# A quarter of the tokens taken out of the dense expert sweep and gathered row by row

## What is computed

```python
idx = e1 * PEER_KEYS + e2                      # 128 tokens x 8 heads x 16
gate = jax.nn.softmax(sc, axis=-1).astype(hb.dtype)
u_sel = u_tab[idx]
v_sel = v_tab[idx]
act = jax.nn.gelu(jnp.einsum('td,thkd->thk', hb, u_sel), approximate=False) * gate
return jnp.einsum('thk,thkd->td', act, v_sel)
```

## Time and profile before

| what | value |
| --- | --- |
| median of 3 runs | 4597.31 us (4595.19 to 4605.93) |
| span of the profiled execution | 4622.7 us, its own time; 0.55% above the median |
| TensorE busy | 94% of the span |
| VectorE, ScalarE, GpSimd busy | 56%, 32%, 42% of the span |
| first to last way-down matmul | 1366.5 to 2707 us of the span |

### The profile page before, as it was taken

The page is one execution under the profiler, slowest core; times in us unless marked ns, Lnnn a source line. Parts: engine busy times, 40 slices in busy tenths (PEclk is TensorE's granted clock), DMA queues, the critical chain, the costliest instruction groups (busy, mean ns, idle before and its releaser), DMA issues.

```text
span 4622.7 us, 51856 instructions
## 1 busy us (share of the span) xinstructions
PE 4338.2 (94%) x20942; PEld 3385.7 (73%) x20942; DVE 2596.0 (56%) x4411; ACT 1498.9 (32%) x2478; POOL 1942.0 (42%) x1058
## 2 busy tenths in 40 slices
PE   7989999998799999999999989988999989989998
PEld 4767755477678888888888866676888867656886
DVE  4785744369857888878544352644434350365334
ACT  4212211035853222222222233553222231353222
POOL 3155332047964555555444433003223226434443
PEclk9989999998899999999999999998999999999999
DMA  7100300332354444444554320001222212102331
GB/s 266 44 23 20 118 30 28 136 112 99 142 205 152 164 167 164 160 164 157 178 166 156 119 69 19 16 15 51 64 64 63 64 34 64 42 1 78 96 93 53
DMA packets 171050, 445.52 MB, mean 96 GB/s; under 512 B 12251, under 2 KB 79003, under 8 KB 167612
## 3 DMA queue, kind: packets, MB, share of 16 engines
q1 hardware_dynamic: 168060, 422.61, 27.3%
q0 software_dynamic: 2752, 19.60, 1.1%
HBM read 404.41 MB, written 37.75 MB: 96 GB/s over the span
## 4 chain that ended last, share of the span: by engine, by line
PE 72%; DVE 3%; POOL 3%; ACT 3%; issue 2%; DMA 0%; POOLq 0%; ACTq 0%; DVEq 0%
PE psum L254 20%; PE psum L256 20%; PE psum L255 20%; PE psum L260 11%; POOL o L1813 1%; PE psum L355 1%; POOL Pe L2685 1%; POOL Pd L2687 1%; DVE o L1696 0%; DVE X L2076 0%; POOL pair L244 0%; ACT o L1765 0%; ACT stage L1771 0%; ACT o L1762 0%; ACT P L2468 0%
## 5 line engine op out<-in xcount | busy, mean ns | idle before, releaser
L244 POOL TENSOR_TENSOR pair<-raw_ring,pair 128x1024 fp32r<-128x1024 f32 x502 | 1306.2, 2611 | 1949.9 <-ACT pair L236 1897.4
L236 ACT CAST pair<-raw_ring 128x1024 fp32r<-128x1024 f32 x502 | 516.1, 1046 | 742.2 <-PE psum L256 708.2
L254 PE MATMUL psum<-pfh,pair 128*128 128x512 f32 x1152 | 459.1, 399 | 4.5 <-DVE pfl L1589 3.5
L255 PE MATMUL psum<-pfl,pair 128*128 128x512 f32 x1152 | 458.0, 398 | 0.0
L256 PE MATMUL psum<-pfh,pair 128*128 128x512 f32 x1152 | 457.9, 397 | 0.0
L1881 DVE SCALAR_TENSOR_TENSOR hlate<-psum,mods,hlate 128x512 f32<-128x512 f32 x512 | 367.8, 748 | 154.2 <-PE psum L256 154.1
L254 PE MATMUL psum<-Ah,pair 128*128 128x512 f32 x1024 | 408.1, 398 | 4.0 <-DVE Al L1875 4.0
L255 PE MATMUL psum<-Al,pair 128*128 128x512 f32 x1024 | 407.8, 398 | 0.0
L256 PE MATMUL psum<-Ah,pair 128*128 128x512 f32 x1024 | 407.8, 398 | 0.0
L254 PE MATMUL psum<-ffh,pair 128*128 128x512 f32 (+1 forms) x1056 | 379.5, 359 | 25.9 <-DVE ffl L2047 15.7
L255 PE MATMUL psum<-ffl,pair 128*128 128x512 f32 (+1 forms) x1056 | 378.5, 358 | 0.0
(11 more groups left out here) (620 smaller groups left out, 8826.7 us busy)
## 6 DMA issues: line engine op xcount, KB each, us to landing
raw_ring<-wmod SPq DMA_DIRECT2D x144, 512.0 KB, 5.5
raw_ring<-peeru SPq DMA_DIRECT2D x128, 512.0 KB, 3.5
raw_ring<-peerv SPq DMA_DIRECT2D x128, 512.0 KB, 3.8
gates<-stage SPq DMA_DIRECT2D x16, 2048.0 KB, 6.6
Gb<-gates SPq DMA_DIRECT2D x32, 1024.0 KB, 9.4
raw_ring<-win SPq DMA_DIRECT2D x48, 512.0 KB, 4.4
raw_ring<-wgate SPq DMA_DIRECT2D x44, 512.0 KB, 3.5
raw_ring<-wup SPq DMA_DIRECT2D x44, 512.0 KB, 3.6
```

The lines of the kernel that those rows point to most:

```text
L236: ac.e.copy(self.pair(t)[0], k.R.of(t)).then_inc(*k.A.up("hi", t))
L244: po.e.tensor_tensor(lo, k.R.of(t), hi.bitcast(F), ALU.subtract).then_inc(*k.G.up("lo", t))
L254: e.matmul(out, w[0], x[0], start=first, stop=False, skip_group_check=True)
L255: e.matmul(out, w[0], x[1], start=False, stop=False, skip_group_check=True)
```

## The change

The last 128 of the 512 tokens leave the dense sweep. `DENSE` is 384.

1. Route: only 96 spreads (three blocks of tokens) instead of 128. For block 3 the expert numbers are written as integers to `row16`, one column for each of its 128 choices, and the block's normalised tokens are turned to rows in `htok` (16 matmuls, two copies).
2. Way up: 8 trios of 384 columns. Its bank is one of two (6 and 7); from tile 17 on the gelu is written back into the bank, and so is the product with the gates (`gelus`, `products`). The gate chunks are 384 wide too.
3. Way down: the roles are turned. 128 tokens of `Ah`/`Al` are the weights, 512 columns of V are streamed; three token blocks by two halves, 18 matmuls of 512 columns a tile, summed over all 128 tiles in six banks. The 512 additions into `hlate` are gone.
4. Rows: for the last 128 tokens, partition = token. GpSimd issues an indirect DMA for each of the 128 choices from the U table and, later, each of the 128 from the V table: 128 rows of 4 KB, 512 KB each, into one of four buffers. VectorE reduces a U row against `htok` (one number per token, first half, groups 0 to 30), and accumulates a V row times its number in `acc` (groups 32 to 62). They are four, at times five a group (128 over 31 groups). GpSimd issues the rows of group `gi+1` in its group `gi`, each after VectorE is done with the row four before it.
5. End: six banks are copied out, 32 transposes bring the tokens back to columns, eight additions into the residual, which is now loaded into `X` once tile 127 is through the way up.

```diff
+DENSE, CHUNKS, SPREADS = 384, 12, 96
...
-    for u in range(128):
+    for u in range(SPREADS):
...
+    def down(n):
+        hi, lo = W.pair(("V", n))
+        pe.wait_ge(W.split(("V", n)), V.at("A", n))
+        for tt, hf in SIDES:
+            ts, hs = slice(128 * tt, 128 * tt + 128), slice(512 * hf, 512 * hf + 512)
+            i = trio(e, B.of(("dense", tt, hf)), (k.Ah[n % 4][:, ts], k.Al[n % 4][:, ts]), (hi[:, hs], lo[:, hs]), n == 0, n == 127)
...
-            project(k, pe, ("U", n), k.px, SEG1)
-        down(gi)
+            project_in(k, pe, ("U", n), k.ux, SEGU, None, (6, 7))
+        down(2 * gi)
+        down(2 * gi + 1)
...
+    def row(s):
+        x = k.sel_rows[s % 4]
+        dv.wait_ge(k.rowl[s % 4].at(s // 4 + 1))
+        if s < 128:
+            dv.wait_ge(A.at("htok", 1))
+            e.tensor_tensor_reduce(x, x, k.htok, 1.0, 0.0, ALU.mult, ALU.add, k.act1[:, s:s + 1]).then_inc(*V.up("row", s))
+            return
...
+        e.scalar_tensor_tensor(out=k.acc, in0=x, scalar=a, in1=k.acc, op0=ALU.mult, op1=ALU.add).then_inc(*V.up("row", s))
...
-        if gi == 63:
-            vector_affine_scale(k, dv, "ev", k.mods2[0], 0, SEG2, P.at("used", ("U", 127)))
-        down(gi)
+            for s in rows[2 * i:2 * i + 2] if i == 0 else rows[2:]:
+                row(s)
...
+    def row(s):
+        po.wait_ge(V.at("row", s - 4) if s > 3 else V.at("rows"))
+        table = k.d["peerrow"] if s < 128 else k.d["peerv"].rearrange("a b c -> (a b) c")
+        at = bass.IndirectOffsetOnAxis(ap=k.row16[:, s % 128:s % 128 + 1], axis=0)
+        e.indirect_dma_start(out=k.sel_rows[s % 4], out_offset=None, in_=table, in_offset=at).then_inc(*k.rowl[s % 4].up())
+
+    for s in chosen_rows(0)[0:4]:
+        row(s)
```

More of the change, by code:

```diff
@@ L1430 @@
 NO, FIRST, EARLY, AHEAD = 4, 8, 14, 17
+DENSE, CHUNKS, SPREADS = 384, 12, 96
+SEGU = [(0, DENSE)]
+SIDES = tuple((tt, hf) for hf in range(2) for tt in range(3))
+GROUPS = 31
 BESIDE = {2: 8, 34: 9, 66: 10}
@@ L1532, in deal @@
     cost, load, out = {"pool": 0.84, "scalar": 0.87, "vector": 0.29}, {"pool": 0.0, "scalar": 0.0, "vector": 0.0}, []
-    for u in range(128):
-        load["vector"] += CHOICE if u < 96 else 0.68
+    for u in range(SPREADS):
+        load["vector"] += CHOICE
         load["scalar"] += 0.58
@@ L1670, in choose @@
         V.name("esel", tt)
+        if tt == 3:
+            dv.wait_ge(V.now())
+            e.scalar_tensor_tensor(out=place, in0=k.esel[:, 0:128], scalar=128.0, in1=k.esel[:, 128:256], op0=ALU.mult, op1=ALU.add).then_inc(*V.up())
+            dv.wait_ge(V.now())
+            e.tensor_copy(k.row16, place).then_inc(*V.up("rows"))
         dv.wait_ge(A.at("gexp", tt))
@@ L1689, in vector_route @@
     dv.wait_ge(V.now())
-    for u in range(128):
+    for u in range(SPREADS):
         tt, n = u // 32, u % NO
         if u % 32 == 0:
-            nxt = choose(tt + 1) if tt < 3 else iter(())
+            nxt = choose(tt + 1)
             dv.wait_ge(V.at("EG", tt))
@@ L1704, in vector_route @@
         next(nxt, None)
-        if u % 32 == 28 and tt < 3:
+        if u % 32 == 28 and tt < 2:
             chosen(tt + 1)
+    for _ in nxt:
+        pass
     V.name("end", "route")
@@ L1772, in spread @@
         B.over(("sp", u), A.now())
+    ac.wait_ge(k.hkeep.at())
+    for hf in range(2):
+        ac.wait_ge(P.at("ht", hf))
+        e.copy(k.htok[:, 512 * hf:512 * hf + 512], B.of(("ht", hf))).then_inc(*A.up("htok", hf))
+        B.over(("ht", hf), A.now())
     choose(0)
-    for u in range(128):
+    for u in range(SPREADS):
         if u in BESIDE:
@@ L1875, in up @@
         e.tensor_tensor(k.Al[n % 4], y, k.Ah[n % 4].bitcast(F), ALU.subtract).then_inc(*V.up("A", n))
[L1877 to L1883, removed]
+        if n >= AHEAD:
+            B.over((("U", n), 0), V.now())
+    def row(s):
[5 more added lines that the diff above has]
+            return
+        a = k.act2[:, s - 128:s - 127]
+        if s == 128:
+            dv.wait_ge(A.at("gelu", "rows"))
+            e.tensor_tensor(k.act2, k.act2, k.gate, ALU.mult).then_inc(*V.up())
+            dv.wait_ge(V.now())
+            e.tensor_scalar(k.acc, x, a, None, ALU.mult).then_inc(*V.up("row", s))
+            return
+        dv.wait_ge(V.at("row", s - 1))
+        e.scalar_tensor_tensor(out=k.acc, in0=x, scalar=a, in1=k.acc, op0=ALU.mult, op1=ALU.add).then_inc(*V.up("row", s))
     def mods(t):
@@ L1971, in pool_experts @@
     for gi in range(NG):
+        rows = [s for s in chosen_rows(gi + 1) + (chosen_rows(gi + 2) if gi + 1 == GROUPS else [])] if gi != GROUPS else []
+        rows = iter(rows)
         for n in ups(gi):
             W.lo(po, ("U", n))
+        for s in rows if gi < 8 else ():
+            row(s)
         for n in (2 * gi, 2 * gi + 1):
+            for s in range(2):
+                nxt = next(rows, None)
+                if nxt is not None:
+                    row(nxt)
             W.lo(po, ("V", n))
+        for s in rows:
+            row(s)
     G.name("end", "experts")
     po.wait_ge(k.V.at("A", 127), k.P.at(("U", 127), 0))
+    e.dma_start(k.X[:, :, 0:512], k.d["hkeep"]).then_inc(*k.hkeep.up())
     e.dma_start(k.X[:, :, 512:768], k.d["ctxT2"]).then_inc(*k.ctxl.up())
@@ L3547, in sync_program @@
     R.load(sp, ("U", FIRST + 7))
-    for ch in range(16):
+    for ch in range(CHUNKS):
         sp.wait_ge(A.at("sp", 8 * ch + 7))
```

150 lines of the change are left out of this document (98 added, 52 removed).

## The result

The changed kernel takes 4432.92 us (median of 4, 4423.59 to 4440.32) against 4598.14 us for the kernel before on the same chip (median of 4). The ratio is 0.963 (95% interval 0.961 to 0.966): 165 us less. Forecast were 4414 us and a ratio of 0.960; the range was 4290 to 4585. In the two profiled executions the spans differ by 191 us (4622.7 and 4431.5). Up to the first scaling of the next block (L2889, now L2992) it is 178 (it starts at 2713.53 and 2535.76); the other 13 lie in later stages with the same instructions in both. That they are the change's is not shown: from that instruction to the end the trace of before takes 1909 us, those of the changed kernel and its eight variants 1889 to 1902. One wait of TensorE of 9.2 us, near 3215, stands in the trace of before and not in that of after; why is open.

The account below looks back on a forecast made before the run. The prediction took TensorE to bound the expert sweep, but not the route, before the change. Sweep -138, route and start -54 and end +9 gave -183 us, from a median of 4597 to 4414 us; range 4290 to 4585.

Parts of the forecast that it names:

- TensorE's price: Expert sweep: matmul time is proportional to columns, 0.176 us for 384; a group of two tiles takes 16.85 us.
- VectorE and the port, groups 8 to 40: Sweep: VectorE's 14.4 us of work plus 6.8 of waits for GpSimd give 21.0 us a group, bounds 19.2 and 23.8.
- Groups 41 to 61: Later sweep: 18.5 us a group with single modulation sums (41 to 56), TensorE's 16.85 with none (from 57).
- Groups 0 to 7: Start of the sweep: VectorE's work and the turning row buffers give 12.2 us a group, 98 us, bounds 80 and 115.
- Group 31 and the rest: Group 31, without rows, takes TensorE's 16.85 us; the whole sweep sums to 1200 us, 138 less.
- fifth rows: Sweep, 8 groups with a fifth row: GpSimd waits into VectorE's next group, 1 us lost each, 8 us.
- Route and start: Before the sweep: 47.3 us of spreads go, 2.41 of wait and 8.2 of ways up saved, issues cost 3.5; together -54.
- End: After the last way down: bank copies, transposes, additions and GpSimd's squares cost +9 us; residual's load has 12 us of cover.
- Rival 1: Sweep: VectorE and GpSimd take turns at the port without cost, TensorE stays the bound; 4221 us, chance 0.10.
- Rival 2: Sweep: an issue and a port operation exclude each other, about 3.5 us a group more on VectorE; 4582 us, chance 0.18.
- Rival 3: Sweep: indirect issues are long, GpSimd becomes the bound; break-even at 2.4 us an issue, 4704 us at 3; chance 0.12.
- Rival 4: Sweep: idling TensorE gets a clock of 0.80, costing up to 3 us in 22 groups, 66; no chance of its own.

Follow-up runs that it names:

- experiment 2: The changed kernel without any gathering of rows and without the rows' arithmetic (256 one-column operations in its place): 4227.61 us, ratio 0.918.
- experiment 1: The changed kernel with the arithmetic of the gathered rows cut to 128 of 1024 columns, every gather and wait kept: 4302.72 us, ratio 0.933.
- experiment 3: The changed kernel with each indirect DMA replaced by a plain GpSimd DMA of 128 neighbouring rows, same bytes and waits: 4392.43 us, ratio 0.954.
- experiment 4: The changed kernel with GpSimd's subtraction cut to 512 of 1024 columns for expert tiles above 40: 4313.44 us, ratio 0.937.
- experiment 5: The changed kernel with GpSimd's list reordered from group 8 on, each subtraction followed by one row issue: 4421.50 us, ratio 0.961.
- experiment 6: The changed kernel with two GpSimd subtractions put before the four first issues and the residual's load issued by ScalarE: 4420.84 us, ratio 0.960.

## Why the prediction was right

The forecast was right in sign, in the mechanism of groups 8 to 40 and nearly in size: 4414 against 4433. Part of the closeness is luck, as terms that were off by 5 to 20 us stand against each other. Point by point:

**TensorE's price.** The way-up matmuls of 384 columns start 0.174 us apart (0.176 taken from half and full width). With nothing beside them a group takes 16.7 us (16.85), experiment 2.

```profile
1603.46 0.34 PE L254 MATMUL psum<-pfh,pair 128*128 128x384 f32 x1
1603.64 0.34 PE L255 MATMUL psum<-pfl,pair 128*128 128x384 f32 x1
1603.81 0.34 PE L256 MATMUL psum<-pfh,pair 128*128 128x384 f32 x1
```

**VectorE and the port, groups 8 to 40.** Forecast: 14.4 us of own work (1.4 of it for ScalarE's rounding) and 6.8 of waits inside instructions, rounded down from 21.2 to 21.0. Measured in groups 8 to 30: instructions of 20.0 us a group, of which 7.3 are above the least length of their kind (5.3 in row sums, 1.9 in modulation sums), so 12.7 of work, and 1.1 of waiting for ScalarE's rounding between; the overlap of ends and starts takes some of it back, and the period is 20.3. A tile's two operations take 0.56 us each; 0.62 was taken. The waits came out at 1.8 a subtraction (1.7 forecast), though in another pattern. The prediction expected row sums at 1.22 or 3.3 us, few between; of the 128 row sums 58 took under 1.35 us, 22 about 1.85 (they met the end of a subtraction), 42 about 3.4, and 6 from 5 to 10, through several subtractions. Experiments 1, 3 and 4 together show that VectorE's work and its waits for the subtractions set the pace, experiment 2 what is left without them.

The Trainium skill ("SBUF — State Buffer", "SBUF: two separate sides") says that whichever starts first keeps the pair for the whole instruction. The trace agrees for a single one. That a waiting VectorE operation was let in only after three of GpSimd's subtractions (1600.38 to 1607.46) goes beyond what that sentence says.

**Groups 41 to 61** were forecast at 18.5 and 16.85 and took 19.2 and 17.8: +16 us together. What was mis-sized is GpSimd's list. The forecast had 1.1 us an indirect issue and its own waits at the port only in subtractions. Measured are 1.37 in the mean (0.93 least; the rest is mostly the wait for VectorE's port operation) and 0.3 us of gap before the next issue. Per group of 41 to 56, 4 x 2.60 + 4.1 x 1.40 + 4.1 x 0.3 = 17.4 us. That is above TensorE's 16.7, but 2.9 of it are waits for VectorE inside the instructions, and up to 19.2 GpSimd stood waiting, mostly for VectorE's rows. So neither list is the bound alone. Experiment 3 takes 1.2 us a group away with plain issues, experiment 1 takes 2.6 away with short row operations and GpSimd's list as it was. VectorE's long instructions there (3.2 us in the mean in 41 to 56, 3.65 in 57 to 61) come from operations that waited through several subtractions; in 41 to 56 there are 14 such, of 7.6 to 8.8 us each; experiment 5 took 2.8 us of waits a group from VectorE and only 0.3 from the period.

**Groups 0 to 7** took TensorE 104.5 us, forecast 98: +6.5. (The table's 14.0 against 12.2 would be +14, but by the same measure the kernel before has 13.0 where TensorE takes 12.2.) Here VectorE did wait for rows (11.7 us in all) and its sums for subtractions; the issues, 1.4 and a gap of 0.3, put more between one row and the next in the same buffer than was assumed. How much each of the two has in it was not separated; with short sums the table's 14.0 was 11.8 (experiment 1).

**Group 31 and the rest.** 14.8 in place of 16.85, as VectorE and TensorE caught up; the 8 us for fifth rows are not visible as such. Together the sweep became 1187.5 us, forecast 1200, 153 less in the trace where 138 were forecast (the sum of before there was 1338, the trace's 1341).

**Route and start.** Forecast -54, measured -43.5 (first way down at 1322.5 against 1366.0; the 1366.5 in the table ahead is half a microsecond late). The mis-sized term is the last 32 spreads. The prediction let them start at 1276.55, but in the trace of before that is the 88th L1696; the 97th starts at 1285.97, so the last 32 take 38.0 us, not 47.3. The spreads start 0.9 us earlier, not 2.4, and the 96 that are left take 4 us less than the first 96 did before (183.4 against 187.3, from the first start to the last). Their end is 43.6 us earlier, where 49.7 was forecast. And the four issues ahead of GpSimd's first subtraction, priced at 3.5, cost 9: from the end of the spreads to the first way down pass 42.1 us, in experiment 6 33.0. The timeline of TensorE:

```profile
1294.77 0.34 PE L256 MATMUL psum<-pfh,pair 128*128 128x384 f32 x1
1301.94 0.69 PE L254 MATMUL psum<-pfh,pair 128*128 128x384 f32 x1 [6.83 <-POOL pair L244]
1302.43 0.53 PE L255 MATMUL psum<-pfl,pair 128*128 128x384 f32 x1
1302.75 0.53 PE L256 MATMUL psum<-pfh,pair 128*128 128x384 f32 x1
```

After 6.8 us of idling the matmuls start 0.32 us apart until 1306, at a granted clock of 0.50 (1.2 GHz); then, at 0.97, they are at 0.174 again. The first issue had in turn waited 6.5 us for the last chunk of gates to be written. With the two subtractions ahead of it (experiment 6) all of it was gone.

**End.** Forecast +9, measured +19, from where the way down ends to the first scaling of the next block (L2889, L2992). TensorE is done at 2510, and VectorE had a stretch of three row operations and a load in its way:

```profile
2499.21 12.66 DVE L1945 SCALAR_TENSOR_TENSOR tok<-selrow,best,tok 128x1024 f32<-128x1024 f32 x3
2511.79 0.24 DVE L2110 TENSOR_SCALAR ones<-mods 128x8 f32<-128x8 f32 x2
2511.94 2.48 DVE L1983 COPY tok<-psum 128x512 f32<-128x512 f32 x4
2518.68 1.41 DVE L1989 SCALAR_TENSOR_TENSOR X<-psum,mods,X 128x512 f32<-128x512 f32 x2 [4.27 <-DMA X<-hkeep]
```

The three take 12.7 us because GpSimd does four subtractions in a row at that time (2498.54 to 2508.01), and the residual's load, which I had "with 12 us of cover", stands behind the same four in GpSimd's list. The cover was counted from way up 127; that the issuing engine would get there in time was assumed. Experiment 6 moved the issue to ScalarE and the wait of 4.3 us went.

**The rivals.** Rival 1, the port hides, did not happen, but its price was right to 7 us (experiment 2). Rival 2, that the issues take part in the contest, was half right: an indirect issue waits for VectorE, VectorE is not made to wait for it, so its 3.5 us a group on VectorE did not come; what came is GpSimd's own time. The row that spoke for it, a plain issue of 0.94 against 0.53, was no such wait by experiment 3, where plain issues took at most 0.58. Rival 3 put the turning point at an issue of 2.4 us; with its gap it is 1.7. Rival 4, the clock: 0.93 to 0.98 granted in the sweep's windows from 1420 us on. It was not tried by itself.

The sum of the errors is start +10, sweep -15, end +10: with them -183 becomes -178, which is what the two traces show up to the first scaling of the next block. Within the sweep, groups 8 to 40 and the fifth rows gave 43 us more than forecast and groups 0 to 7, 31 and 41 to 63 took about 30 back (by TensorE's own starts). The two spans differ by 191 and the medians by 165 only, because the profiled execution of before was 25 us above its median and that of after was not.

## What to carry to other kernels

When work is moved from the engine that is the bound to others, add up not only each engine's own time but the use of what two of them share: here 4 x 2.35 + 8.13 x 1.14 us a group at the SBUF port of VectorE and GpSimd gave 18.7 us, the kernel took 20, and no busy share of an engine would have shown it. The sum is a lower bound and no forecast: with short row operations it is about 15, and the groups took 18 to 19 (experiment 1). A wide spread in the length of one instruction (1.2 to 10 us) was such a wait here; keeping one operand in PSUM took it away (the gate product, 0.551 to 0.566 us). And for each DMA that is moved to another queue, ask what stands in front of it there, not only from when its data could be loaded: two such places cost 12 us here (experiment 6).

## What the runs showed of the hardware that was not expected

A VectorE operation with two SBUF inputs that waits for GpSimd is not always let in between back to back subtractions: it waited through three of them, 6.3 us, and in the worst case, through four, took 10.15 us instead of 1.21. Whether it is let in goes with what the subtraction that it meets went through. Over the nine traces with whole subtractions, it was let in at once in all 367 cases in which that subtraction had been held up itself; where it had not, it waited to the end of the series in 129 cases and was let in at once in 37, 25 of these in the run without rows; it was never let in halfway. The connection is seen, its cause is not known.

An indirect DMA of 128 rows of 4 KB takes GpSimd 0.93 us, up to 1.98 when VectorE holds the port, and 0.3 us pass before a second one behind it starts. The exclusion is one-sided: VectorE's sums keep their 1.21 us under an issue. A plain DMA of GpSimd took 0.53 to 0.58 us beside the same VectorE operations (experiment 3), so it is not kept waiting, and 21 of them began as the one before ended, without the gap of 0.3 us.
